# Value loads regrouped, first weight split earlier, one row_sum buffer, form loads on another queue: a stick-breaking attention stage on one core

## The reference

```
h = rms_norm(x, norm_g)
u_pool, z_pool, q, k, v, z_attn, gate_logits = split(h @ w_in)
y_pool = multiscale_pool(u_pool) * silu(z_pool)
# attention, for 16 blocks of 128 queries, each head:
logits = q_blk @ k.T / sqrt(64)
log_beta, log_1m_beta = log_sigmoid(logits), log_sigmoid(-logits)   # causal, s < t
later  = reverse_cumsum(log_1m_beta) - log_1m_beta
attn   = exp(log_beta + later) @ v
y_attn = attn * silu(z_attn)
merged = gate0 * (y_pool @ w_pool_up) + gate1 * (y_attn @ w_attn_up)
x = x + merged @ w_out ;  out = rms_norm(x, final_g)
```

## Time and profile before

| | before |
|---|---|
| time, median of 3 runs | 1638.39 us (1637.9 to 1639.77) |
| the profiled execution | 1638.39 us, its span 1636.6 us |
| mean granted PE clock | 0.994 |
| PE busy | 1588.0 us, 97% |
| DVE busy | 1134.4 us, 69% |
| POOL busy | 905.3 us, 55% |
| ACT busy | 756.2 us, 46% |
| bytes moved | 228.82 MB, mean 140 GB/s |

### The profile page before, as it was taken

The page is one execution under the profiler, slowest core; times in us unless marked ns, Lnnn a source line. Parts: engine busy times, 40 slices in busy tenths (PEclk is TensorE's granted clock), DMA queues, the critical chain, the costliest instruction groups (busy, mean ns, idle before and its releaser), DMA issues. The chain is left out here.

```text
span 1636.6 us, 24903 instructions
## 1 busy us (share of the span) xinstructions
PE 1588.0 (97%) x8030; PEld 1321.5 (81%) x8030; DVE 1134.4 (69%) x1554; ACT 756.2 (46%) x1448; POOL 905.3 (55%) x665
## 2 busy tenths in 40 slices
PE   8999999999999999999999999999999899999998
PEld 6877888788888887888877888888887678888886
DVE  6745424764989889998888988999887763333323
ACT  4411222224666665676665666666666431112111
POOL 3421102421789878888777897898874332314140
PEclk9999999999999999999999999999999999999999
DMA  7733335754434252452793333434314773534332
GB/s 248 234 127 119 130 116 182 252 161 144 142 94 112 81 141 83 115 141 76 248 318 113 107 98 101 117 93 134 105 42 142 218 229 110 164 110 149 115 103 77
DMA packets 150867, 228.82 MB, mean 140 GB/s; under 512 B 46929, under 2 KB 72017, under 8 KB 150754
## 3 DMA queue, kind: packets, MB, share of 16 engines
q1 hardware_dynamic: 146722, 212.73, 42.5%
q10 hardware_dynamic: 4032, 14.68, 2.5%
HBM read 149.76 MB, written 77.60 MB: 139 GB/s over the span
## 5 line engine op out<-in xcount | busy, mean ns | idle before, releaser
L1593 DVE TENSOR_TENSOR_SCAN left<-keep,left 128x512 f32<-128x512 f32 x192 | 296.5, 1544 | 32.7 <-issue 20.4
L1412 PE MATMUL psum<-hT,ring 128*128 128x512 f32 x644 | 264.3, 410 | 6.2 <-DMA hT<-form_scratch 3.0
L1660 POOL TENSOR_TENSOR ring<-raw,ring 128x512 fp32r<-128x512 f32 x138 | 232.9, 1688 | 59.8 <-ACT ring L1492 45.2
L1416 PE MATMUL psum<-hT,ring 128*128 128x512 f32 x644 | 263.0, 408 | 0.0
L1414 PE MATMUL psum<-hT,ring 128*128 128x512 f32 x644 | 262.3, 407 | 0.0
L1498 ACT ACTIVATE keep<-psum 128x512 f32<-128x512 f32 (+3 forms) x320 | 170.8, 534 | 177.6 <-PE psum L1438 175.2
L1505 ACT ACTIVATE wt<-psum 128x512 fp32r<-128x512 f32 (+3 forms) x320 | 171.2, 535 | 111.6 <-PE psum L1446 108.7
L1458 PEld LDWEIGHTS psum<-wt,vm 128*128 128x128 f32 x1088 | 171.0, 189 | 32.7 <-issue 7.0
L1599 DVE TENSOR_TENSOR wt<-psum,wt 128x512 fp32r<-128x512 f32 (+3 forms) x320 | 189.8, 593 | 8.9 <-ACT wt L1505 6.4
L1458 PE MATMUL psum<-wt,vm 128*128 128x256 f32 x1088 | 182.0, 282 | 5.2 <-DVE row_sum L1608 4.4
L1446 PE MATMUL psum<-ident,left 128*128 128x128 f32 x1088 | 170.9, 272 | 1.4 <-DVE wt L1599 1.3
(11 more groups left out here) (181 smaller groups left out, 3234.8 us busy)
## 6 DMA issues: line engine op xcount, KB each, us to landing
raw<-in_w_strips SPq DMA_DIRECT2D x92, 256.0 KB, 4.1
qm<-qk_scratch SPq DMA_DIRECT2D x128, 128.0 KB, 4.2
gate<-gate_scratch SPq DMA_DIRECT2D x64, 256.0 KB, 3.9
hT<-form_scratch ACTq DMA_DIRECT2D x28, 512.0 KB, 6.5
xt<-in_x SPq DMA_DIRECT2D x16, 512.0 KB, 5.1
xT<-in_x_T SPq DMA_DIRECT2D x16, 512.0 KB, 4.2
qk_scratch<-staging SPq DMA_DIRECT2D x32, 256.0 KB, 2.6
qk_scratch<-store_lo SPq DMA_DIRECT2D x32, 256.0 KB, 3.5
```

The costliest lines, as they stand in the source:

```text
L1412: pe.matmul(o, hi, m_hi, start=k == 0, stop=False)
L1416: last = pe.matmul(o, lo, m_hi, start=False, stop=k == HK - 1)
L1593: dve.tensor_tensor_scan(left[:, n % LN, span][:, ::-1], k, k, carry, ALU.mult, ALU.bypass).then_inc(scanned, 1)
L1660: pool.tensor_tensor(out_, a, b, op).then_inc(s, 1)
```

## The change

Six edits, all in `stage3`.

1. `V_LOAD` is now at the earliest twelve steps ahead of a unit's first item and one step behind the rounding of the unit before; `V_HI` is three steps instead of four behind the load. For the four units that are loaded in the first half these were the steps 13, 26, 35 and 40, rounded at 17, 30, 39 and 44; they are now 28, 32, 36 and 40, rounded at 31, 35, 39 and 44. The same table repeats every 40 steps, seven times. The last of each four doesn't move.
2. `FIRST_SPLIT` is gone, so the first weight tile has the step 2 instead of 6; all others keep theirs.
3. `row_sum` has one buffer instead of two, and `add_halves` waits for the row before.
4. The 28 form loads are issued by SP instead of ACT, at the same steps.
5. SP issues, within a step, key, value, query loads instead of key, query, value loads.
6. `store_y` comes two steps earlier.

The orders of PE and DVE don't change.

```
-        V_LOAD.append(max(K_LAST[u - VN] + AV_LAG - 3, V_HI[u - 1] + 1) if u >= VN else 0)
-        V_HI.append(max(V_LOAD[u] + 4, K_LAST[u - VN] + AV_LAG + 1) if u >= VN else 0)
+        V_LOAD.append(max(K_FIRST[u] - SOON, V_HI[u - 1] + 1) if u >= VN else 0)
+        V_HI.append(max(V_LOAD[u] + 3, K_LAST[u - VN] + AV_LAG + 1) if u >= VN else 0)
...
-    FIRST_SPLIT = fin[1] + 5
-    W_STEP = [max(step, FIRST_SPLIT) for step in steps_of(split(GROUPS, 0), split_step)]
+    W_STEP = steps_of(split(GROUPS, 0), split_step)
...
-    row_sum = sb("row_sum", [P, 2, 2 * P])
+    row_sum = sb("row_sum", [P, 2 * P])
...
 (in SP's block)
+            def load_form(j, kk):
+                hold(part_done, SWITCH + j + 1)
+                sp.dma_start(hT[:, HOME[j], kk, :, :].bitcast(F32), form_d[j, kk]).then_inc(form_in[j], DMA)
...
+                for u in at(V_LOAD, s):
+                    if u >= NC:
+                        load_v(u)
                 for u in at(Q_LOAD, s):
                     if u >= 2:
                         load_q(u)
-                for u in at(V_LOAD, s):
-                    if u >= NC:
-                        load_v(u)
...
+                for j in range(FORMS):
+                    for kk in range(HK):
+                        if s == FORM_STEP[j, kk]:
+                            load_form(j, kk)
...
-                    if item(n)[1] % 4 == 0 and s == n + AV_LAG + 4:
+                    if item(n)[1] % 4 == 0 and s == n + AV_LAG + 2:
                         store_y(n)
...
 (in ACT's block: load_form and its loop go)
...
 (in DVE's block)
-                wait(dve, y_done, row - 1)
+                wait(dve, y_done, row)
```

More of the change, by code:

```diff
@@ L1525, in take @@
                 act.activation(sum_a if j == A11 else sum_c, bank_p(part(g, j)), ACT.Copy).then_inc(taken, 1)
-            def load_form(j, kk):
-                act.wait_ge(part_done, SWITCH + j + 1)
-                act.dma_start(hT[:, HOME[j], kk, :, :].bitcast(F32), form_d[j, kk]).then_inc(form_in[j], DMA)
             def value_hi(u):
@@ L1562, in _ @@
                     high_part(s - T_LAG)
[L1563 to L1566, removed]
                 for u in at(V_HI, s):
@@ L1606, in add_halves @@
                 dve.wait_ge(half_done, row + 1)
-                wait(dve, y_done, row - 1)
-                dve.scalar_tensor_tensor(row_sum[mine, row % 2, :], bank_o(row)[mine, :], v_ends[mine, n // NI, i:i + 1],
+                wait(dve, y_done, row)
+                dve.scalar_tensor_tensor(row_sum[mine, :], bank_o(row)[mine, :], v_ends[mine, n // NI, i:i + 1],
                                          half_sum[mine, :], ALU.add, ALU.add).then_inc(row_done, 1)
@@ L1700, in finish_row @@
                     wait(pool, y_stored[u % 2], u // 2, DMA)
-                step(y_out[mine, u % 2, i % 4 * P:i % 4 * P + P], row_sum[mine, row % 2, 0:P],
-                     row_sum[mine, row % 2, P:2 * P], ALU.add, y_done, row + 1)
+                step(y_out[mine, u % 2, i % 4 * P:i % 4 * P + P], row_sum[mine, 0:P],
+                     row_sum[mine, P:2 * P], ALU.add, y_done, row + 1)
             def value_diff(u):
```

## The result

The changed kernel takes 1677.24 us (median of five runs, 1675.17 to 1681.85) against 1638.01 for the kernel before: ratio 1.0246, 95% interval 1.0228 to 1.0265 (the two medians alone give 1.0240). The forecast was 1680.5 in a range of 1652 to 1704. The profiled execution took 1680.16 us with a span of 1678.4 us, 41.8 more than before.

What follows compares the result with a forecast made beforehand. The prediction took TensorE (PE), with work in 97% of the span, as the bound. Its terms, 8.1 + 17 + 8 + 12 - 3 = 42.1 us, on 1638.4 gave 1680.5 us, range 1652 to 1704.

Steps and rivals of the forecast that it cites:

- PE has no slack, so a wait is not won back: Whole span: TensorE (PE) has work in 97% of it, so any wait that reaches it is paid in full.
- Opening, 8.1: First weight split near 411 us: ACT waits for weight blocks, PE idles 6.4 us plus 1.7 of half clock.
- Value clusters, 17 + 8: Four value-load clusters: late POOL hand-overs delay query loads, 17 us over the first three and 8 at the fourth.
- One row_sum buffer, 12: Late half ends: DVE waits for POOL's previous row, so PE waits for row_sum three times, 4 us each.
- Form loads, -3: Form loads moved to SP: the last can go earlier, removing PE's 2.8 us wait, -3 us.
- Store, 0: Earlier y_out store: SP waits sooner for the same POOL instruction; taken as 0, between -1 and +4 us.
- The clock: Half clock after PE stalls: 1.7 us priced once, at the opening; none priced at the other new stalls.
- rival F: Each new stall drops the clock: seven more tolls of 1.7 us, 12 us, about 1692; chance 0.05.
- overlap (A): Waits overlap as POOL catches up while PE stalls, row_sum terms vanish: 21 us, about 1659; chance 0.22.
- Feeding each other (B): Late SP, POOL and DVE delay one another, terms at 1.6 times: 64 us, about 1702; chance 0.15.
- the queue rule (C): Query loads between 790 and 865 stand behind 512 KB forms: +7 us, form gain gone, 1688; chance 0.12.
- D: Faster: SP runs ahead, value loads not late, first weight blocks land before ACT needs them: about 1631; chance 0.03.

Runs made afterwards that it cites:

- the form run: The kernel before with only the form loads moved from ACT to SP; ratio 0.9996 (0.9987 to 1.0006), -0.7 us.

## Why the prediction was right

The time came out 3.3 us under the forecast, and the loss lies in the eight places that were named. That it came so near is in part luck: two errors of about 15 us cancel, as the last step below shows. By its steps:

- **PE has no slack, so a wait is not won back.** Right. Between the clusters the lateness stays constant to 0.1 us over 20 items (items 50 to 70 and 130 to 150).
- **Opening, 8.1.** Right: 8.7 in the trace, 8.0 alone.
- **Value clusters, 17 + 8.** Right in sum (17.4 + 7.9 in the trace, 23.3 alone) and in the chain. Why the hand-overs are late, POOL being three steps behind, is borne out by the run with the loads from step 22. The first clusters hold 5.7 us of slow clock that I hadn't priced, so their idle time was forecast too long: 17 against 11.7 measured; in the fourth it was 8 against 5.0. The chain was read as one path ending at the query load. The run with the query first shows a second, through ACT and DVE, which keeps 8.6 of 15.5 us in the first three clusters.
- **One row_sum buffer, 12.** Right in kind, a little too large: 8.9 in the trace, 10.3 and 11.1 by the runs. PE was to wait for row_sum itself, well over 4.4 us; that wait is 0.3 us, and it waits for `sum_d` behind it (10.8). The buffer also binds in the first halves (4.04 us at 503.99), which the forecast left out.
- **Form loads, -3.** 1.9 us in the trace, nothing that a run can tell.
- **Store, 0.** It was +3.0, in the bounds.
- **The clock.** This is the term that was wrong in size. I priced one stall with 1.7 us and left the others to rival F, at a chance of 0.05. They paid 13.5 us over the other seven stretches, close to the 12 of rival F. The idle time was overestimated by 15.8: the terms without the toll were 43.4 us, and 27.6 were measured. The two errors nearly cancel. The Trainium skill, "TensorE: Matmul & The Clock Gate" (Part 1: The HAM clock gate), says that idling halves the clock until activity releases it. Seven of eight stretches of the changed kernel show granted clocks of 0.87 to 0.97, and in the kernel before one did (0.97), so the trace agrees more than I had let it.

Of the rivals, overlap (A) with its 21 us in all is refuted; what overlaps is 3.6 us or nothing. Feeding each other (B), 64 us, is refuted by the parts that add up to 43.9, and the 7 us of the queue rule (C) by the form run. F had the toll right and the idle time not. D ended at the opening as said.

## What to carry to other kernels

Price a hand-over between engines by how late its slowest engine is at that step, and not by its distance in the program alone: the same value code cost nothing with loads at steps 22, 26 and 31, and 23 us at 28, 32 and 36. When an engine without slack stalls, add a slow clock behind the stalls; here it was a third of the loss (15.3 of 42.9 us). And when a wait is taken away, look for a second chain from the same late point before expecting the gain.

## What the runs showed of the hardware

- The clock's toll doesn't follow the idle time. In the third cluster 2.6 us of new idle time cost 0.5 us of clock, in the second 4.0 us cost 2.7. In the last stretch (items 270 to 290) both kernels idle 2.7 to 2.9 us; before paid nothing and the changed kernel 1.2.
- Small loads in a full stretch are slow, with the 512 KB form loads on the other queue or on the same. The 128 KB pieces of the query loads issued between 801 and 820 us landed after 5.1 to 10.4 us in the kernel before (forms on ACT) and 5.6 to 9.9 with the forms on SP; the longest was 13.6, with the later store. The median of the whole execution is 4.2.
